# Output projection of a hybrid decoder trunk: products over the first six heads, for four of eight units, moved into the last head's attention steps

## The reference

```python
q = apply_rope(q, cos, sin)
k = apply_rope(k, cos, sin)
# per block of 128 queries, 8 heads, c = 0, 1:
s = jnp.einsum('bqhcd,bkhcd->bhcqk', qb, k) * scale      # causal mask
p = jax.nn.softmax(s, axis=-1)
attn = p[:, :, 0] - lam_full * p[:, :, 1]
o = jnp.einsum('bhqk,bkhe->bqhe', attn, v)
o = rms_norm(o, subln_gain) * (1.0 - lambda_init)        # per head, 128 wide
h = h + o.reshape(bsz, L, D_MODEL) @ w_o
hn = rms_norm(h, norm_ffn_gain[i])
h = h + conv_ffn(hn, ...)
```

## Time and profile before

| | us |
|---|---|
| median of 3 runs (lowest, highest) | 1514.13 (1513.78, 1515.37) |
| profiled run, its own time | 1514.71 |
| span of the profiled execution | 1512.9 |
| PE busy | 1324.0 (88% of the span) |
| DVE, ACT, POOL busy | 912.6, 535.6, 692.9 |
| mean granted clock of TensorE | 0.929 |

### The profile page before, as it was taken

How to read it: one execution, slowest core, us unless ns; L and a number is a source line. 1 busy time by engine, 2 the same in 40 slices (tenths; PEclk the granted TensorE clock), 3 DMA queues, 4 the chain that set the end, 5 groups by cost and what they waited for, 6 DMA issues and landing times.

```text
span 1512.9 us, 27145 instructions
## 1 busy us (share of the span) xinstructions
PE 1324.0 (88%) x10620; PEld 1252.4 (83%) x10620; DVE 912.6 (60%) x1093; ACT 535.6 (35%) x870; POOL 692.9 (46%) x395
## 2 busy tenths in 40 slices
PE   3245364999999999999999999998999999999996
PEld 2245354899999999999988787875999999999996
DVE  5988888222788888812145565555358888884001
ACT  4222122343334434322254554543223433431322
POOL 4855444466444444466554343340563444443341
PEclk9567667899999999999999999995999999999998
DMA  7021111333232233232321111110223223223232
GB/s 147 5 38 29 36 21 27 89 96 96 62 106 83 83 97 97 77 104 88 108 70 56 43 44 55 43 43 14 70 72 96 83 86 108 83 83 88 77 91 80
DMA packets 205960, 108.71 MB, mean 72 GB/s; under 512 B 7543, under 2 KB 204808, under 8 KB 205832
## 3 DMA queue, kind: packets, MB, share of 16 engines
q1 hardware_dynamic: 201796, 105.81, 25.1%
q10 hardware_dynamic: 4101, 2.05, 0.6%
HBM read 101.55 MB, written 2.10 MB: 69 GB/s over the span
## 4 chain that ended last, share of the span: by engine, by line
PE 47%; issue 19%; DVE 14%; POOL 12%; ACT 6%; ACTq 1%; DMA 0%; DVEq 0%; POOLq 0%
PE ps L290 33%; POOL wL L277 9%; PE ps L821 4%; PE ps L944 2%; PE ps L853 1%; DVE Kp L1455 1%; DVE tmpE L1445 1%; ACT u L1217 1%; PE ps L680 1%; DVE tmpE L1429 1%; DVE T L1444 1%; PE ps L658 1%; ACT wH L273 1%; POOL qk L1924 1%; POOL sqt L1877 1%
## 5 line engine op out<-in xcount | busy, mean ns | idle before, releaser
L277 POOL TENSOR_TENSOR wL<-raw,wH 128x1024 fp32r<-128x1024 f32 (+1 forms) x184 | 444.2, 2426 | 666.8 <-ACT wH L273 665.7
L290 PE MATMUL ps<-hgH,wH 128*128 128x264 f32 (+1 forms) x1408 | 285.4, 284 | 1.1 <-DVE hgL L1532 1.1
L290 PE MATMUL ps<-hgH,wL 128*128 128x264 f32 (+1 forms) x1408 | 285.3, 284 | 0.0
L290 PE MATMUL ps<-hgL,wH 128*128 128x264 f32 (+1 forms) x1408 | 285.0, 284 | 0.0
L273 ACT ACTIVATE wH<-raw 128x1024 fp32r<-128x1024 f32 (+1 forms) x184 | 186.1, 1039 | 195.7 <-PE ps L290 143.9
L290 PEld LDWEIGHTS ps<-hgH,wH 128*128 128x128 f32 x1408 | 218.9, 189 | 1.4 <-issue 1.3
L290 PEld LDWEIGHTS ps<-hgL,wH 128*128 128x128 f32 x1408 | 218.4, 189 | 0.0
L290 PEld LDWEIGHTS ps<-hgH,wL 128*128 128x128 f32 x1408 | 217.8, 189 | 0.0
L290 PE MATMUL ps<-actH,wH 128*128 128x264 f32 (+1 forms) x960 | 193.8, 283 | 2.2 <-POOL wL L277 2.0
L290 PE MATMUL ps<-actL,wH 128*128 128x264 f32 (+1 forms) x960 | 193.2, 282 | 0.0
L290 PE MATMUL ps<-actH,wL 128*128 128x264 f32 (+1 forms) x960 | 193.0, 282 | 0.0
(11 more groups left out here) (300 smaller groups left out, 2174.8 us busy)
## 6 DMA issues: line engine op xcount, KB each, us to landing
raw<-ffn_w_up SPq DMA_DIRECT2D x88, 512.0 KB, 3.7
raw<-ffn_w_down SPq DMA_DIRECT2D x32, 512.0 KB, 4.1
raw<-attn_w_qkv SPq DMA_DIRECT2D x24, 512.0 KB, 3.8
raw<-s_w_glu SPq DMA_DIRECT2D x16, 512.0 KB, 3.9
raw<-ffn_w_down SPq DMA_DIRECT2D x16, 384.0 KB, 3.4
TT<-Kp SPq DMA_DIRECT2D x64, 64.0 KB, 2.5
raw<-attn_w_o SPq DMA_DIRECT2D x8, 512.0 KB, 3.9
X<-x SPq DMA_DIRECT2D x1, 2048.0 KB
```

The lines of the kernel that those rows point to most:

```text
L277: nc.gpsimd.tensor_tensor(wL[:, slot, 0:nk], raw[:, slot % 2, 0:nk], wH[:, slot, 0:nk].bitcast(F32), ALU.subtract).then_inc(w_lo, 1)
L290: mm = nc.tensor.matmul(ps[:, bank + b, 0:tw], w[:, slot, k, :], x[:, kt, t0:t0 + tw], start=first and k == 0 and s0, stop=last and k == n ...
```

## The change

Of units 0 to 3 of the output projection, the products over k = 0 to 5 (heads 0 to 5) run inside head 7's steps 0 to 3, unit i in step i, always in banks 6 and 7 (`wo_part`): k 0 to 3 ahead of the step's attention product, k 4 and 5 behind it. In steps 0 to 2 they cover only the 512 real tokens (spans of 256, `FROM16`), and DVE adds each sum to `hT` inside the step (`add_part`, which waits for `wo_ps` and frees the banks by `wo_free`). Unit 3 covers all tokens and stays in its banks. For units 0 to 2 the 16 meta columns over k 0 to 5 are made apart, 18 products of 16 columns each (`wo_meta`). `out_projection` on PE is written out: k = 6 of units 3, 0 and 1, the turn of head 7, k = 7 of units 0 and 1, then units 2 and 3, then units 4 to 7 whole. The banks of the units are given by `wo_bank`. `first_turned` moves from bank 7 to bank 4, behind the wait for `v_set`. DVE's part of the output projection is unrolled; ACT's, POOL's and SP's code is unchanged.

```diff
@@ -238,6 +238,9 @@
             return ps[:, 2 if h < HEADS - 2 else h - (HEADS - 2)]
         vt = u[:, 0, 2:2 + L]
+
+        def wo_bank(n):
+            return (4, 2, 0, 6, 4, 6, 2, 0)[n]
         def unit_bank(n):
             return 2 if n == 2 else 4 + 2 * ((n + (n > 2)) % 2)
@@ -460,6 +463,8 @@
         mask_set = sem("mask_set")
         head_in = sem("head_in")
         first = sem("first")
+        wo_ps = sem("wo_ps")
+        wo_free = sem("wo_free")
         sc_ps = sem("sc_ps")
         row_ps = sem("row_ps")
         max_set = sem("max_set")
@@ -886,7 +891,7 @@
             def first_turned():
                 pe.wait_ge(first, 4)
                 for h in range(HEADS):
-                    mm = nc.tensor.transpose(ps[0:META, 7, h * META:(h + 1) * META], A0[:, h],
+                    mm = nc.tensor.transpose(ps[0:META, 4, h * META:(h + 1) * META], A0[:, h],
                                              ident[0:META, 0:META])
                 mm.then_inc(first, 1)
@@ -932,12 +937,14 @@
                     unit_part(v_next, 5, 7)
                 elif i == 3 and more_q:
                     unit_part(q_next, 1, 5)
+                if h == HEADS - 1:
+                    wo_part(i, 0, 4)
+                if i == 0:
+                    pe.wait_ge(v_set, h + 1 + FREE)
                 if n == NS - NQ:
                     first_turned()
                 if n == NS - NQ + 2:
                     first_back()
-                if i == 0:
-                    pe.wait_ge(v_set, h + 1 + FREE)
                 pe.wait_ge(at_set, n + 1)
                 for t in (*range(1, i + 2), 0):
                     kn = TILES[t][1]
@@ -956,6 +963,8 @@
                     v_transposes(h + 1)
                     if more_q:
                         unit_part(q_next, 5, 8)
+                if h == HEADS - 1:
+                    wo_part(i, 4, 6)
                 if n == NS - NQ - 2:
                     first_scores()
                 if n == NS - NQ:
@@ -976,19 +985,56 @@
                 for n in range(NS):
                     attend(n // NQ, n % NQ)
+            def wo_products(n, bank, kts, spans, start=False, stop=False):
+
+                for k in kts:
+                    pe.wait_ge(o_hi, k + 1)
+                    pe.wait_ge(o_lo, k + 1 + FREE)
+                    for w, x, s0, s1 in ((wH, oH, True, False), (wH, oL, False, False), (wL, oH, False, True)):
+                        for b, (t0, tw) in enumerate(spans):
+                            mm = nc.tensor.matmul(ps[:, bank + b, 0:tw], w[:, n % 4, k, :], x[:, k, t0:t0 + tw],
+                                                  start=start and k == kts[0] and s0,
+                                                  stop=stop and k == kts[-1] and s1)
+                return mm
+
+            def wo_part(n, k0, k1):
+
+                if k0 == 0:
+                    pe.wait_ge(w_hi, U_WO + n + 1)
+                    pe.wait_ge(w_lo, U_WO + n + 1)
+                    if n == 0:
+                        pe.wait_ge(first, 2)
+                    else:
+                        pe.wait_ge(wo_free, n)
+                    if n == NQ - 1:
+                        pe.wait_ge(first, 13)
+                last = n < NQ - 1 and k1 == HEADS - 2
+                mm = wo_products(n, 6, range(k0, k1), FROM16 if n < NQ - 1 else ALL, k0 == 0, last)
+                if last:
+                    mm.then_inc(wo_ps, 1)
+
+            def wo_meta(n, bank):
+
+                wo_products(n, bank, range(HEADS - 2), ((0, META),))
+
             def out_projection():
-                def ready(kt):
-                    if kt == 0:
-                        pe.wait_ge(first, 13)
-                    if kt == HEADS - 1:
-                        turn_head(HEADS - 1)
-                    pe.wait_ge(o_hi, kt + 1)
-                    pe.wait_ge(o_lo, kt + 1 + FREE)
-                for n in range(CT):
-                    if n >= 4:
-                        pe.wait_ge(h_new[2], n - 3 + FREE)
-                    unit_products(pe, U_WO + n, n % 4, 2 * ((n + 2) % 4), oH, oL, ALL, 0, 8, True, True,
-                                  ready if n == 0 else None)
+                wo_products(3, 6, (HEADS - 2,), ALL)
+                pe.wait_ge(first, 13)
+                wo_products(0, wo_bank(0), (HEADS - 2,), ALL, start=True)
+                wo_meta(0, wo_bank(0))
+                pe.wait_ge(o_set, NS)
+                wo_products(1, wo_bank(1), (HEADS - 2,), ALL, start=True)
+                wo_meta(1, wo_bank(1))
+                turn_head(HEADS - 1)
+                for n in range(2):
+                    wo_products(n, wo_bank(n), (HEADS - 1,), ALL, stop=True).then_inc(w_used, 1)
+                wo_products(2, wo_bank(2), (HEADS - 2,), ALL, start=True)
+                wo_meta(2, wo_bank(2))
+                for n in (2, 3):
+                    wo_products(n, wo_bank(n), (HEADS - 1,), ALL, stop=True).then_inc(w_used, 1)
+                for n in range(4, CT):
+                    pe.wait_ge(h_new[2], (1, 4, 2, 3)[n - 4] + FREE)
+                    unit_products(pe, U_WO + n, n % 4, wo_bank(n), oH, oL, ALL, 0, 8, True, True)
                 pe.wait_ge(h_new[2], CT - 2 + FREE)
             glu()
@@ -1685,6 +1731,8 @@
                     head_rest(h - 2)
                 if n == NS - 2:
                     head_rest(HEADS - 2)
+                if h == HEADS - 1 and i < NQ - 1:
+                    add_part(i)
                 if n == NS - NQ - 1:
                     first_difference()
                 if n == NS - NQ:
@@ -1728,7 +1776,7 @@
             def first_copied():
                 dve.wait_ge(first, 5)
-                V.tensor_copy(AT0[:, :], ps[0:META, 7, 0:HEADS * META]
+                V.tensor_copy(AT0[:, :], ps[0:META, 4, 0:HEADS * META]
                               .rearrange("p (h q) -> p h q", q=META)).then_inc(first, 1)
             def first_squares():
@@ -1770,15 +1818,18 @@
                 head_norm(HEADS - 1)
                 head_rest(HEADS - 1)
+            def add_part(n):
+
+                dve.wait_ge(wo_ps, n + 1)
+                o = span(hT[:, n], FROM16)
+                V.tensor_tensor(o, o, pspan(3, FROM16), ALU.add).then_inc(wo_free, 1)
+
             def out_projection():
-                with dve.Fori(0, 2) as i:
-                    for m in range(4):
-                        n = i * 4 + m
-                        dve.wait_ge(w_used, n + (U_WO + 1))
-                        V.tensor_tensor(span(hT[:, ds(n, 1)].rearrange("p a t -> p (a t)"), ALL),
-                                        span(hT[:, ds(n, 1)].rearrange("p a t -> p (a t)"), ALL),
-                                        pspan((m + 2) % 4, ALL), ALU.add).then_inc(h_new[2], 1)
-                        split_gain(2, n, i * 4 + (GAIN_FFN + 8 + m), n + 1)
+                for n in range(CT):
+                    dve.wait_ge(w_used, U_WO + n + 1)
+                    o = span(hT[:, n], ALL)
+                    V.tensor_tensor(o, o, pspan(wo_bank(n) // 2, ALL), ALU.add).then_inc(h_new[2], 1)
+                    split_gain(2, n, GAIN_FFN + 8 + n, n + 1)
             def add_down(l, ct, used, m, spans):
                 dve.wait_ge(w_used, used)
```

## The result

| | before | after |
|---|---|---|
| median of 7 runs each (lowest, highest) | 1514.70 (1513.78, 1515.97) | 1519.69 (1517.04, 1521.39) |
| ratio to before, 95% interval | | 1.0031 [1.0019, 1.0043] |
| profiled run; span | 1514.71; 1512.9 | 1520.08; 1518.3 |
| mean granted clock | 0.929 | 0.927 |

The forecast was 1514.6 with a range of 1507 to 1519. A later comparison on another chip gave 1519.39 and 1.0028 [1.0018, 1.0038]. The loss is real, about 5 us in the first and 4.2 in the second.

What follows compares the result with a forecast made beforehand. It took head 7 to be bound by small handovers, partly at half clock, and the tail by PE, then GpSimd after the change. +7.2 us before the tail and -6.7 in it gave +0.5, so 1514.6, range 1507 to 1519.

Steps and rivals of the forecast that it cites:

- Bound: Before the change: head 7 is a ring of small handovers, partly at half clock; in the tail PE is the bound.
- Part 2 (step 0): Head 7, step 0: first_output starts 4.3 us later, behind DVE's new add and AT0 copy; the clock falls.
- Part 3, steps 1 to 3: Head 7 after step 0: clock returns around step 1's 24 products; last attention product ends 1069.4, against 1060.5 before.
- the small products at 0.065 us: Products on the 16 meta columns: 0.065 us each, with 0.044 and 0.122 kept as bounds; 36 cost 2.3 us.
- Part 1: Work taken out of the tail: 132 products now run before head 7's attention product ends; 54 small ones are new.
- T: Point where the last head's products begin: 1070.51 before, forecast 1077.7, +7.2 us.
- Part 4, the tail: From T to S: 46.9 us in place of 53.6, -6.7, set by GpSimd and the hgL wait; PE's need 39.2.
- S: Point of the statistics product, 1124.13 before; forecast near 1124.6, with nothing different behind it.
- The sum: Whole kernel: +7.2 for T and -6.7 for the tail give +0.5 us, so 1514.6.
- Half clock stays through step 2: Rival in head 7: clock still 0.50 at step 2's start, +5.0 us, T +12.2, time 1519.6; chance 0.15.
- Clock holds: Rival in head 7: clock does not fall, T only +0.8 us, time 1508.2; chance 0.30.
- Tail in full: Rival in the tail: squares and loads run ahead, S - T is 39.2 to 41, time 1508.7; chance 0.05.

Runs made afterwards that it cites:

- e4: Changed kernel with head 7's turn issued earlier and step 0 reordered (first_output ahead of k 4 and 5, AT0 copy directly behind Ob): 1509.43, ratio 0.9958.
- e5: Changed kernel with the 54 narrow products made 256 columns wide in place of 16, same count and weight loads: 1517.55, ratio 1.0022.
- e1: Changed kernel without the 54 products on the 16 meta columns, all else the same: 1514.70, ratio 0.9996.
- e7: Changed kernel with the squares of the output projection's units made by ACT, GpSimd only adding them up: 1519.04, ratio 1.0026.
- c2: Kernel before with only DVE's loop over the output projection's eight units written out, same order and banks: 1514.36, ratio 1.0001.

## Why the prediction was wrong

**Bound, and Part 2 (step 0): right.** `first_output` 4.2 us later, forecast 4.3, behind DVE's copy, which stands behind the new add. The first fall of the clock came, too. e4 shows that it was avoidable: 7.5 in place of 11.3.

**Part 3, steps 1 to 3: right** within 0.4 us, the return of the clock included.

**The step that failed: the small products at 0.065 us** in Part 1, carried into Part 3 as "36 small, 2.3". They took 8.72 - 30 x 0.122 = 5.1 us. The step took the price of the turn of the meta outputs, a product with as few columns (16), for theirs. The halving for the clock was nearly right, as this turn after the change shows, at full clock, in the chain that ended last:

```profile
1061.02 0.59 PE ps L908 x8
```

That is 0.074 each. The neighbour was the wrong one: its stationary tile has 128 columns as well, but 16 rows, and that of the narrow products 128 rows. e5 shows that the moving columns hardly count (16 or 256: 0.111 or 0.116). So the stationary side is left as the likely reason, but no run changed it alone. The range's upper bound, 0.122, did cover the price. The Trainium skill, "TensorE: Matmul & The Clock Gate", section on LDWEIGHTS, has it in a load of 107 ns for each, against 0.111 measured at full clock. The same section says that the rows don't matter; by that the neighbour would have cost 107 ns too, and it took 0.074, with loads of 0.136 us where those of the narrow products last 0.19. So that part of the rule does not agree with this trace. (The prediction's sentence by that page has 36 x 0.042 as 1.6; it is 1.5, which makes 1516.1.) At half clock a narrow product took 0.213, close to twice as much.

**What was missing altogether: a second fall of the clock, in a busy engine.** The prediction asked only whether gaps would lower the clock in step 0. None of the rows read from before has 18 narrow products in a line, so nothing warned; but the text never asked what such a run would do. With both: 36 x 0.111 is 1.7 more than taken, the last 9 of them at half clock 0.9, the turn at half clock 0.5, together 3.1 of the 3.4 us by which T was late (forecast +7.2, measured +10.6).

**Part 4, the tail: right number, wrong cause.** Forecast 46.9, set by GpSimd and `hgL` with PE waiting; measured 46.4, with PE never waiting. That the two agree is luck. PE's own need was put at 39.2, which leaves out six products: behind T stand k = 7 of four units and k = 6 of unit 2, 30 wide products and not 24 (the chain's 48 are these and 18 narrow ones). With 0.7 for the six, 0.8 for the price of the 18, and 5.7 for the first 56 products at half clock (12.3 us for what takes 38 x 0.122 + 18 x 0.111 = 6.6), PE's need is 46.4. GpSimd ended its eighth round at 1127.8, 0.8 ahead of S, so both bounds lay within a microsecond of each other. That is why e1, free of the second fall, still gains nothing on before, and why e7 gains nothing either. The waits that the prediction named are shown by e1.

**The sum.** Forecast +0.5; T 3.4 more, tail 0.5 less, gives S +3.4; with 0.9 at the end +4.3, against 5.0 and 4.2 in the two comparisons.

**The rivals.** "Half clock stays through step 2" named 1519.6, the time that came, but not the mechanism: the clock was back at 1.00 when step 2 began. Its price stood at the wrong place, so the 0.15 was no foresight. "Clock holds" (1508.2) did not come in the changed kernel. "Tail in full" did not come: S - T was 46.4, and e1 shows the waits that it denied.

## What to carry over

In this kernel a product with a 128 x 128 stationary tile took 0.111 to 0.122 us at full clock, whether it moved 16 columns or 264, so splitting one into a wide and a narrow part nearly doubles its price. Count such products, not columns, and take a price from a row whose stationary tile is of the same shape. When work is moved, list every run of unusual instructions that the new order makes, and ask of each what it does to the clock, also where the engine never idles. And where a turn or a handover has independent products behind it, issue it ahead of them: that one line was worth 2 us in the kernel before.

## What the runs showed of the hardware that was not expected

- The granted clock fell from 1.00 to 0.50 while PE was busy for 3.00 of 3.00 us with 16-column products (1075 to 1078 after the change); with 256 columns in the same products it stayed at 1.00 (e5).
- Eight products with a stationary tile of 16 rows and 128 columns took 0.074 us each at full clock, those with one of 128 rows and 128 columns 0.111, both with 16 moving columns. The first are transpositions; the turn of a head, also transpositions, has 128 rows and takes 0.44 for four, 0.11 each.
- `hgL` (two inputs in SBUF, 128x528) took 0.77 to 2.35 us. The slowest began 0.6 us after GpSimd had begun a weight split; the fastest began as one GpSimd operation ended, and the next on GpSimd then took 1.79 us instead of 1.32. Rows of DVE, then of GpSimd, in the changed kernel:

```profile
1085.64 2.35 DVE L1578 SCALAR_TENSOR_TENSOR hgL<-hT,PV,hgH 128x528 fp32r<-128x528 f32 x1 [1.02 <-ACT hgH L1191]
...
1115.56 0.77 DVE L1578 SCALAR_TENSOR_TENSOR hgL<-hT,PV,hgH 128x528 fp32r<-128x528 f32 x1 [3.57 <-ACT hgH L1191]
```

```profile
1085.06 2.37 POOL L280 TENSOR_TENSOR wL<-raw,wH 128x1024 fp32r<-128x1024 f32 x1 [64.06 <-ACT wH L276]
...
1115.72 1.79 POOL L1929 TENSOR_TENSOR acc<-acc,sqt 128x528 f32<-128x528 f32 x1
1126.51 1.32 POOL L1929 TENSOR_TENSOR acc<-acc,sqt 128x528 f32<-128x528 f32 x1
```

  The Trainium skill, "SBUF — State Buffer", section "Who interferes with whom", says that a DVE instruction with two SBUF inputs contends with a GpSimd instruction that reads SBUF, and that the order of issue decides who waits. These rows agree.
- The place of an instruction fetch moved from 1501.6 to 1513.4 when DVE's loop was written out (c2).
